# One spread matmul a token in the passes, the gate's three parts side by side and added by VectorE; the gathered rows dealt anew in turns of 16 tiles

## The reference, cut to what matters

```
e = i1 * N_KEYS + i2                       # expert number, N_KEYS = 128
g = jax.nn.softmax(sc, axis=-1)            # gate of each chosen expert
z = jnp.einsum('thkd,td->thk', u[e], h)    # dot with the expert's down row
a = jax.nn.gelu(z) * g
out = jnp.einsum('thk,thkd->td', a, v[e])  # sum of the experts' up rows
```

## Time and profile before

| what | us |
|---|---|
| median of 3 runs (4013.39 to 4025.32) | 4022.35 |
| the profiled execution's own time | 4017.01 |
| its span | 4015.2 |
| layer 0: rounds, 747.0 to 877.6 | 130.6 |
| layer 0: pass 0, to 1064.2 | 186.6 |
| layer 0: pass 1, to 1334.2 | 270.0 |
| layer 0: pass 2, to 1601.4 | 267.2 |
| layer 0: pass 3, to 1823.0 | 221.6 |
| layer 1: the same stages, 2903 to 3983 | 1080 |

### The profile page before, as it was taken

One profiled execution on the slowest core, in us unless ns is written; L12 is line 12 of the kernel. 1 busy time (PEld: TensorE's weight loads), 2 busy tenths in 40 slices (PEclk: granted clock), 3 DMA queues, 4 the chain that ended last, 5 costly groups with the idle time before them and its releaser, 6 DMA issues.

```text
span 4015.2 us, 51259 instructions
## 1 busy us (share of the span) xinstructions
PE 3550.4 (88%) x16134; PEld 2172.7 (54%) x16134; DVE 2344.3 (58%) x4758; ACT 1226.5 (31%) x3175; POOL 656.8 (16%) x602
## 2 busy tenths in 40 slices
PE   7977998559999999996998999799437999999997
PEld 3443583235567677663444544357334466677664
DVE  1072688478878655564122500258978877755556
ACT  1141010356644444001011100111156654544201
POOL 0000001133334211220000000000132333311221
PEclk9998999659999999998998999899758999999998
DMA  3101138659999877993221122213557999978897
GB/s 132 64 21 53 63 137 355 230 208 366 360 390 405 345 313 313 397 382 146 73 73 47 42 73 73 84 54 124 227 213 292 368 372 392 405 314 313 349 383 282
DMA packets 129888, 926.82 MB, mean 231 GB/s; under 512 B 14800, under 2 KB 15744, under 8 KB 18184
## 3 DMA queue, kind: packets, MB, share of 16 engines
q0 software_dynamic: 73728, 536.90, 33.6%
q1 hardware_dynamic: 52368, 377.51, 24.5%
q10 hardware_dynamic: 3704, 11.36, 0.8%
HBM read 923.59 MB, written 2.12 MB: 231 GB/s over the span
## 4 chain that ended last, share of the span: by engine, by line
PE 82%; DVE 9%; issue 5%; DMA 2%; ACT 2%; DVEq 0%; ACTq 0%; SPq 0%; POOLq 0%
PE proj L647 22%; PE proj L433 17%; PE obk L638 17%; PE proj L425 10%; PE tps L596 9%; PE proj L611 3%; PE proj L582 1%; DMA wring<-in_slabs 1%; DVE xn L1369 1%; DVE ring L1324 1%; DVE ring L1352 1%; PE obk L746 1%; PE tps L398 1%; DVE hT L1394 0%; DVE ring L1326 0%
## 5 line engine op out<-in xcount | busy, mean ns | idle before, releaser
L647 PE MATMUL proj<-wring,hT 128*128 128x512 f32 x2048 | 948.2, 606 | 1.2 <-DVE hT L1404 1.2
L378 POOL DMA_INDIRECT ring<-in_experts,idx x512 | 629.6, 1230 | 1745.4 <-DVE xn L1369 1634.6
L638 PE MATMUL obk<-hT,wring 128*128 128x256 f32 x3072 | 694.2, 379 | 0.0
L638 PEld LDWEIGHTS obk<-hT,wring 128*128 128x128 f32 x3072 | 583.6, 190 | 159.5 <-issue 89.2
L1369 DVE SCALAR_TENSOR_TENSOR xn<-ring,coef,xn 128x1024 f32<-128x1024 f32 x512 | 628.7, 1281 | 22.4 <-DVE coef L1359 1.2
L1352 DVE SCALAR_TENSOR_TENSOR ring<-ring,xn 128x1024 f32<-128x1024 f32 x512 | 602.6, 1222 | 27.5 <-DMA ring<-in_experts,idx 27.2
L596 PE MATMUL tps<-hT,hot 128*128 128x32 bf16 x6144 | 409.5, 238 | 226.1 <-issue 138.8
L647 PEld LDWEIGHTS proj<-wring,hT 128*128 128x128 f32 x2048 | 383.1, 195 | 383.0 <-issue 376.8
L433 PE MATMUL proj<-hT,wring 128*128 128x512 f32 x1280 | 562.2, 597 | 9.5 <-DMA ring<-in_keys 5.5
L922 ACT ACTIVATE hot<-iotab,away 128x128 bf16<-128x128 bf16 x1792 | 548.8, 392 | 2.3 <-issue 0.8
L596 PEld LDWEIGHTS tps<-hT,hot 128*128 128x128 bf16 x6144 | 379.8, 118 | 306.6 <-issue 178.5
(11 more groups left out here) (233 smaller groups left out, 2120.6 us busy)
## 6 DMA issues: line engine op xcount, KB each, us to landing
wring<-in_slabs SPq DMA_DIRECT2D x356, 1024.0 KB, 7.2
ring<-in_experts,idx POOLq DMA_INDIRECT x512, 8.7
x_res<-in_x SPq DMA_DIRECT2D x1, 2048.0 KB, 10.0
ring<-in_keys ACTq DMA_DIRECT2D x2, 1024.0 KB, 6.5
out<-x_res SPq DMA_DIRECT2D x4, 512.0 KB, 2.6
ring<-ada_rows ACTq DMA_DIRECT2D x1, 1536.0 KB, 6.4
ring<-in_norm_pre ACTq DMA_DIRECT2D x2, 512.0 KB, 9.3
ring<-ada_rows ACTq DMA_DIRECT2D x1, 1024.0 KB, 17.2
```

The source lines that it names most:

```text
L378: pool.indirect_dma_start(rows[:, r, :], None, d[f"experts{layer + 1}"], bass.IndirectOffsetOnAxis(idx[:, k, r:r + 1], 0)).then_inc(row[r] ...
L638: m = pe.matmul(obk[:, j % 2, 0:DT], wring[:, k, at + c * P:at + (c + 1) * P], hT[:, c, GB * P:T], start=(c == 0), stop=(c == DC - 1))
L647: m = pe.matmul(proj[:, 2 * b + c, :], coef_t[:, j % 2, b * P:(b + 1) * P], wring[:, k, at + c * 512:at + (c + 1) * 512], start=False, sto ...
```

## The change

The edits, all inside the expert layers:

1. **Spread in passes 0 to 2.** `spread_parts` does one matmul a token with the three parts side by side, 96 columns, and no accumulation: 8 matmuls a group. The output of a group takes both halves of `tps` (`sided`), so a group waits until the one before it is read (`spread_free >= grp + 2`, it was `grp + 1`).
2. **VectorE takes the result.** `parts_sum`, last in VectorE's work of a tile, waits for the group's matmuls and adds the three parts by one `tensor_reduce` out of PSUM (8 x 32 outputs, 3 inputs each, 32 floats apart). ScalarE's `spread_take` is gone from the passes, and so is its wait for `coef_t_ready` in pass 0.
3. **Table by key.** For chunks 2 and 3 the table is written key by key, so that `tile_coefs` reads 256 floats that lie together; for chunks 0 and 1 it reads every 32nd float, as before.
4. **The rounds.** They keep the three matmuls. VectorE makes 3 tokens of `hot2` (`ON_DVE`), ScalarE 5, and ScalarE takes a group's result after it has made `hot2` of the next group, not before.
5. **Rows dealt anew.** The loops of the passes turn over 16 tiles; `PASS_UNITS` is (2, 6, 5, 5), so the passes take 4, 12, 10 and 10 units (they took 8, 12, 8 and 8). The sums of a half unit come one tile behind its dots.

```diff
-PASS_UNITS = (2, 3, 2, 2)
+ON_DVE = 3
+TURN = 16
+PASS_UNITS = (2, 6, 5, 5)
...
 def row_dots_at(c, j):
-    if PASS_UNITS[c] == 2:
-        return (j // 2,) if j % 2 == 0 else ()
-    return (j // 4 * 3 + j % 4,) if j % 4 < 3 else ()
+    n = 2 * PASS_UNITS[c]
+    return [q for q in range(n) if q * TURN // n == j]
...
+            def spread_parts(grp, k):
+                pe.wait_ge(hot_ready, grp + 1)
+                pe.wait_ge(hot2_ready, grp + 1)
+                pe.wait_ge(spread_free, grp + 2)
+                for t in range(TG):
+                    m = pe.matmul(sided[:, t, 0:PARTS * CK].rearrange("p (c n) -> p c n", c=PARTS), hot2[:, k, t, :],
+                                  hot1[:, :, k, :, t], start=True, stop=True)
+                m.then_inc(spread_done, 1)
...
-                        hot2_group(layer, 0, n, g % 2, token, range(TG // 2, TG))
-                        spread_take(layer, 0, n, g % 2, token)
+                        hot2_group(layer, 0, n, g % 2, token, range(ON_DVE, TG))
+                        if g or not first:
+                            spread_take(layer, 0, n - 1, (g + 1) % 2, token - TG)
...
-                            if c == 0:
-                                act.wait_ge(coef_t_ready, tile + (layer * TILES + 1 + 2))
-                            if c + 1 < CHUNKS:
-                                spread_take(layer, c + 1, tile, j % 2, token)
...
+            def parts_sum(layer, c, g, token):
+                v.wait_ge(spread_done, g + ((layer * CHUNKS + c) * SGROUPS + 1 + 2))
+                parts = sided[:, :, 0:PARTS * CK]
+                if c == 1:
+                    v.tensor_reduce(spread[:, 1, bass.ds(token, TG), :], parts.rearrange("p t (c n) -> p t n c", c=PARTS),
+                                    AX, ALU.add).then_inc(spread_free, 1)
+                else:
+                    v.tensor_reduce(by_key[:, c % 2, :, bass.ds(token, TG)], parts.rearrange("p t (c n) -> p n t c", c=PARTS),
+                                    AX, ALU.add).then_inc(spread_free, 1)
...
                             for q in row_dots_at(c, j):
                                 row_dots(layer, it * PASS_UNITS[c] + (FIRST_UNIT[c] + q // 2), q % 2)
+                            if c + 1 < CHUNKS:
+                                parts_sum(layer, c + 1, tile, it * (TURN * TG) + j * TG)
```

More of the change, by code:

```diff
@@ L54 @@
 RGROUPS = SGROUPS // ROUNDS
-PASS_UNITS = (2, 3, 2, 2)
-FIRST_UNIT = [ROUTED + ROUNDS + STEPS // 2 * sum(PASS_UNITS[:c]) for c in range(CHUNKS + 1)]
+ON_DVE = 3
+TURN = 16
+PASS_UNITS = (2, 6, 5, 5)
+FIRST_UNIT = [ROUTED + ROUNDS + CK // TURN * sum(PASS_UNITS[:c]) for c in range(CHUNKS + 1)]
 assert FIRST_UNIT[CHUNKS] == UNITS and SGROUPS == BODY * STEPS
@@ L146, in build @@
         obk = ps("obk", [P, 2, 512])
+        sided = tps[:, :, :].rearrange("p k n -> p (k n)").rearrange("p (t n) -> p t n", t=TG)
         def part(t, at, n):
@@ L156, in build @@
         coef_t = hT[:, 2:4, 0:DT]
+        by_key = part(ring, NRING, NSPREAD).rearrange("p (k n t) -> p k n t", k=2, t=DT)
         first_z = part(ring, NRING + NSPREAD // 2, CK * DT).rearrange("p (i t) -> p i t", t=DT)
@@ L630, in spread_step @@
                         n = it * BODY + j
-                        spread_group(n + (layer * CHUNKS + c) * SGROUPS, j % 2)
+                        spread_parts(n + (layer * CHUNKS + c) * SGROUPS, j % 2)
                 def dots_tile(tile, j):
@@ L974, in experts, with spread_round @@
                 act.wait_ge(tr_free, job + 2)
-                with act.Fori(0, ROUNDS) as it:
+                def spread_round(it, first):
                     for g in range(RGROUPS):
@@ L988, in experts @@
                         late_loads(layer)
[L989 to L992, removed]
+                    with act.Fori(0, CK // TURN) as it:
+                        for j in range(TURN):
+                            tile = it * TURN + j
+                            token = it * (TURN * TG) + j * TG
                             if c:
@@ L1389, in hot_group @@
                 if both:
-                    half = [P, TG // 2, NK]
-                    v.tensor_tensor(hot2[:, k, 0:TG // 2, :], bcast(iotab[:, :], 1, half),
-                                    bcast(keys[:, 1, bass.ds(token, TG // 2)], 2, half), ALU.is_equal)
+                    some = [P, ON_DVE, NK]
+                    v.tensor_tensor(hot2[:, k, 0:ON_DVE, :], bcast(iotab[:, :], 1, some),
+                                    bcast(keys[:, 1, bass.ds(token, ON_DVE)], 2, some), ALU.is_equal)
                 v.wait_ge(hot1_set, g + (first + 1))
@@ L1404, in tile_coefs @@
                 v.tensor_tensor(coef_t[:, j % 2, :], z,
-                                spread[:, c % 2, :, bass.ds(key, 1)].rearrange("p t n -> p (t n)"),
+                                spread[:, c, :, bass.ds(key, 1)].rearrange("p t n -> p (t n)") if c < 2 else
+                                by_key[:, c % 2, bass.ds(key, 1), :].rearrange("p n t -> p (n t)"),
                                 ALU.mult).then_inc(coef_t_ready, 1)
@@ L1451, in experts @@
                         v.wait_ge(mm_done, 4 * first + CK - 1)
-                    with v.Fori(0, STEPS // 2) as it:
-                        for j in range(2 * BODY):
-                            tile = it * (2 * BODY) + j
+                    with v.Fori(0, CK // TURN) as it:
+                        for j in range(TURN):
+                            tile = it * TURN + j
                             if c + 1 < CHUNKS:
-                                hot_group(layer, c + 1, tile, j % 2, it * (2 * BODY * TG) + j * TG)
+                                hot_group(layer, c + 1, tile, j % 2, it * (TURN * TG) + j * TG)
                             tile_coefs(layer, first, c, tile, j)
```

8 lines of the change are left out of this document (5 added, 3 removed).

## The result

The changed kernel takes 4217.11 us (median of 4 runs, 4203.19 to 4226.49) against 4020.57 (4013.39 to 4025.32) for the kernel before: a ratio of 1.0488, 95% interval 1.0453 to 1.0522. Slower was forecast, but 4044; the time lies far outside the range of 3982 to 4125. The profiled execution took 4213.60, with a span of 4211.8, which is 196.6 over that of before.

A forecast was written before the change was run, and what follows sets the result against it. It took ScalarE's closed loop to bound rounds and pass 0, TensorE passes 1 to 3, DMA close behind. Per layer -34 + 61 - 4 - 23 + 11 = +11, +22 in all: 4039, as median 4044 us, range 3982 to 4125.

The forecast's parts named there:

- Rounds: Rounds: taking behind the next `hot2` opens ScalarE's loop, leaving VectorE the bound at 2.98 us a group; 34 us saved a layer.
- Pass 0, the loop: Pass 0: a new closed loop through VectorE, spread to `parts_sum`, `hot_group`, `tile_coefs`, `sum_tile`; 6.89 us a tile over 5.64.
- I take 0.075: Spread in passes: assumed spacing in us of the 96-column matmuls, making the link from spread to its reader 0.94 us.
- Pass 0, the clock: Pass 0: TensorE idles 2.7 us a tile, so its clock falls to 1.2 GHz in some tiles, costing 1.69 us each.
- I take half, 27 us: Pass 0: the clock assumed to fall in half the tiles, between 3 in 64 and every tile (54 us a layer).
- Pass 0, no limit elsewhere: Pass 0: row work hidden, ScalarE out of the loop, DMA no limit, so taking units out gains nothing.
- the rival of 1.52: `parts_sum`: strided PSUM read costs what it does in SBUF, 1.52 us instead of 0.95; kernel 4112, chance 0.28.
- Pass 2: Pass 2: TensorE's sum falls to 242 us, above DMA's 227 and VectorE's 214; 244 us taken, 23 saved.
- Pass 1: Pass 1: limits of 242 (TensorE), 250 (VectorE) and 256 us (DMA); 266 taken with waits for rows, 4 saved.
- Pass 3: Pass 3: two more units make DMA the limit at 227 us, 233 with unevenness; 11 us longer.
- Columns, not issue: Spread matmuls: columns set the spacing (0.178 us), TensorE gains nothing, pass 0 is 27 us longer; kernel 4152, chance 0.06.
- the clock falls in every tile: Pass 0: TensorE's clock falls in all tiles, 27 us a layer more; kernel 4098, chance 0.08.

The follow-up runs named there:

- experiment 6: Kernel before with only the rounds' edit (VectorE 3 tokens of `hot2`, ScalarE 5, take behind the next `hot2`): 3941.51 us, ratio 0.9807.
- experiment 2: Changed kernel with the 96-column spread matmul reading packed columns (runs of 32, wrong values) instead of every 8th bf16: 4002.33 us, ratio 0.9964.
- experiment 8: experiment 6 plus ScalarE's take behind the next `hot2` in pass 0, and `hot1` packed for three narrow matmuls in the passes: 3872.02 us, ratio 0.9633.
- experiment 3: Changed kernel with eleven extra matmuls that nobody reads behind each spread in pass 0, to keep TensorE busy: 4096.71 us, ratio 1.0202.
- experiment 5: Changed kernel with row units dealt as before the change, 8, 12, 8 and 8 in the passes: 4199.17 us, ratio 1.0457.
- 10: Changed kernel with spread ahead of `sum_tile` in pass 0, and `hot1` as in experiment 8, read by one matmul of 96 packed columns: 3909.20 us, ratio 0.9747.
- experiments 4: Changed kernel with `parts_sum` copying only the first of the three parts instead of adding them: 4205.99 us, ratio 1.0461.
- experiment 1: Changed kernel with TensorE's spread ahead of `sum_tile` in pass 0, and one wait more in `parts_sum`: 3966.35 us, ratio 0.9875.

## Why the prediction was wrong, by its own steps

The miss is 197 - 22 = 175 us of span. Pass 0 holds 106 of it, pass 2 36, pass 1 29, and all else 4.

- **Rounds: right.** -34 a layer against -34.5 and -34.6; the fourth edit alone is worth 78 us (experiment 6).
- **Pass 0, the loop: named rightly, first link mis-sized.** The step that failed is "I take 0.075", the spacing of the new matmuls. It was 0.169, and the link 1.70 us instead of 0.94. 0.77 us on 64 tiles is 49 us. The evidence taken, that the spacing is also 0.06 at the low clock, speaks against columns at the array's clock. It doesn't speak against a read that takes 1.8 ns a column at either clock, and by experiments 2 and 8 the step of that read is what sets it. The prediction itself had weighed the price of a strided read with VectorE's 608 ns, and did not look at the moving operand, whose index `[:, :, k, :, t]` has the token innermost.
- **Pass 0, the clock: named rightly, mis-sized.** "I take half, 27 us" a layer: it fell in 49 of 64 tiles, and the full price was 2.6 us, not 1.69. 51 and 61 us, confirmed by the 47 and 56 of experiment 3. That is 58 us more than taken. Both terms together, 107 us, are the whole miss of the pass. The prediction summed them as if they were apart, and they are not: in experiment 2 the gap is as long, only the spread is shorter, near the forecast's 0.6 us, and the clock costs 18 us in both layers, not 112 and not the 54 taken. So by experiment 2 the taken half would not have come true with the matmul as forecast either. Why the clock holds there is open.
- **Pass 0, no limit elsewhere: right.** DMA share 0.38 with fewer units. Units put back moved it by +21 and -4, which goes with the clock (experiment 5).
- **`parts_sum`: right**, 955 ns against 0.95, and the rival of 1.52 fell.
- **Pass 2: the same mis-sized matmul.** PE is busy 264.70 of 264.70, a tile is 8.26 us, of which the spread has 1.35; before it had 1.43. The 0.83 us that the change was to save were 0.08. Packed columns bring 25 to 35 us where 23 were forecast: 235.2 / 238.1 (experiment 2), 239.2 / 243.5 (10).
- **Pass 1: wrong sign, from two terms.** The first is again the mis-sized matmul: TensorE saved nothing, where 0.83 us a tile were taken. The second is a path left out. The prediction took the largest of three sums, 256 us of DMA, and put 10 on it for rows not yet landed. It had no term for VectorE's row dots holding back ScalarE's `hot2` and so TensorE, and that wait is all of TensorE's idle time there, 11.7 and 16.2 us. With packed columns, where TensorE has the most room, it grows to 33 to 36 us, and the pass takes 282 to 285 if VectorE takes the table (experiments 2 and 10), 267 to 270 if ScalarE does (8). None of the three sums gives this order: with 227, 243 and 259 us of work on VectorE (experiments 4, 2 and 10) layer 0 takes 277, 285 and 282 us. What in `parts_sum` lengthens the chain is open.
- **Pass 3: right**, +11.5 and +9.2; with the two units taken out again TensorE is full (experiment 5).
- **The cases.** "Columns, not issue" had 0.06 and "the clock falls in every tile" 0.08. Both came true, or nearly, in the same run. Their prices above the forecast were 108 and 54: 4044 + 108 + 54 = 4206, 11 us from the time measured. That this lies so close is partly luck. The spacing of 0.169 is near the 0.178 of the first case for another reason, since packed columns take a quarter of it, and the clock fell in 49 tiles at a higher price, not in 64. They were handled as rivals that exclude each other, and the range ended at 4125, below even the first alone (4152). They do not exclude each other: experiment 2 removes the first and most of the second, experiment 3 the second alone. That the kernel got slower at all was not luck: the loop named for pass 0 is there, and experiment 1 opens it.

## What to carry to other kernels

Before counting matmuls, read the access pattern of the moving operand: with its elements 16 bytes apart a column cost about 1.8 ns, and fewer, wider matmuls saved nothing; packing them, with the narrow matmuls left as they were, saved the 0.83 us a tile that the rewrite was to save. An instruction that one engine needs from another belongs ahead of the long piece of work that can hide the answer; here the order of two lines was worth 246 us. A sum for each engine doesn't show a chain that runs through three of them; the waits of the bounding engine do. And cases that can come true together need their sum inside the range.

## What the runs showed of the hardware that was not expected

- A gap of 2.6 us before every `sum_tile` brought TensorE's clock down in 49 of 64 tiles with strided spreads (1.53 us busy) and in 10 of 64 with packed ones (0.50 us busy), and a gap of 2.04 in 61 of 64, each counted in one execution. Filled with matmuls to 0.21 us, it fell only in the first tile of each layer. Which of the patterns keeps the clock up could not be told from the gap's length.
- VectorE reads PSUM with elements 32 floats apart at full rate in a reduce (955 ns for 768), but pays in SBUF: `tile_coefs` takes 609 ns for 256 floats in pass 2 before the change and 419 after it, where the table lies together.
- VectorE multiplies 768 bf16 elements in 0.56 us, and in 958 ns in the layout of experiment 8, where one operand is repeated along the innermost dimension.
- Packed, a matmul of 32 columns stands 0.025 us from the next and one of 96 columns 0.041; strided they stood 0.059 and 0.169 apart.
